# A fused two-layer transformer step on one core: the order of the last three expert blocks and of the work around their gate-up matmuls

## The chip, the cores and the metric

One core of a Trainium2 chip. The metric is the device time of one execution of the whole kernel in microseconds (us), the median over runs.

## The reference

Two layers over 384 tokens (three tiles of 128: one tile of context tokens, two of latent tokens) of width 1024. Each layer has a mixer (retention, windowed attention and neighbourhood attention with one input and one output projection) and then a mixture of experts. The change lies in the second part:

```python
xp = layer_norm(ALPHA * xp + g1 * y, ln1_g[l], ln1_b[l])
f = moe_ffn(xp * (1.0 + sc2) + sh2, w_router[l], b_router[l], w_expert_gu[l],
            w_expert_down[l], w_shared_gu[l], w_shared_down[l])
xp = layer_norm(ALPHA * xp + g2 * f, ln2_g[l], ln2_b[l])
...
def expert_block(args):
    tok, e = args
    gu = x[tok] @ w_gu[e]
    return (jax.nn.silu(gu[:, :D_EXPERT]) * gu[:, D_EXPERT:]) @ w_down[e]
```

There are 64 experts of hidden width 256 (gate-up weights of 2 MB and down weights of 1 MB each), and each token goes to 6 of them. All 64 experts' weights are read from HBM in each layer, so a layer moves about 201 MB in this part. The sum f of a token is its six weighted expert rows and a shared expert's row.

## The kernel before

**Blocks.** The experts are ranked by how many tokens they have, and packed by rank into NB = 29 blocks of 128 rows (`plan_blocks`). A block of one kind holds one expert (128 rows), of another two (64 rows each), a third kind three experts (64, 32 and 32 rows), a fourth two (96 and 32). The experts have a load number n in the order in which blocks use them, 0 to 63. In the kernel before, the last blocks hold: block 24 loads 53 to 55, block 25 loads 56 and 57, block 26 loads 58, 59 and 60, block 27 loads 61 and 62, block 28 load 63.

**A block's work.** For block b: POOL gathers the 128 token rows from memory (L2187); PE transposes them (`turn_rows`, L1118), ACT copies them out (L2099, L2100); PE multiplies by gate and up (`gate_up`, L1141); ACT takes silu (L2107) and DVE the product with the slot's weight (`hidden`, L1617); PE transposes that (`turn_hidden`, L1153), DVE copies (`hidden_turned`, L1626); PE multiplies by down into banks 5 and 6 (`down_rows`, L1168); ACT takes the high part of the two halves (`rows_high`, L2115) and DVE the low part (`rows_out`, L1849). Then the rows are summed back to tokens by a 0/1 matrix (`token_rows`, L1822): six units (three token tiles times two halves f of 512 columns), each unit two matmuls, of the high and of the low part. For blocks 0 to 25 (`add_rows`, L1193 and L1194), PE writes a unit into a bank and DVE adds it to the accumulator in SBUF (`add_unit`, L1835). For the last three (KEPT = 26, 27, 28; `sum_rows`, L1218 and L1219) the six units are kept in six banks (SUM_BANK) and PE accumulates over the three blocks.

**The steady loop.** In iteration b PE runs, in program order: `gate_up(b)`, `add_rows(b-2)` four units, `turn_rows(b+1)`, the other two units, `down_rows(b-1)`, `turn_hidden(b)`. Each engine runs its own list in order; semaphores join them.

**The queue of SP.** The gate-up weights lie in a ring of NG = 4 buffers, the down weights in ND = 6. SP asks for load n of gate-up (L704) when the gate-up matmuls of the block that used load n-4 are done, and for down weights n (L708) when the down matmuls of the block that used load n-6 are done, both in one list in program order: for each b first the down weights of block b, then the gate-up weights whose buffer block b freed. In layer 0 the first two chunks of the next layer's input projection follow (L759), when the blocks of loads 60 and 61 are done.

**The end of a layer.** After `gate_up(28)` PE does units 0 and 1 of block 26's sum, `turn_hidden(28)`, a branch on a value in SBUF (taken only if an expert has more tokens than its room; not taken here), `down_rows(27)`, the rest of block 26's sum, `down_rows(28)`, the sums of block 27 and of block 28. DVE: `gate_sum(0)` to `gate_sum(2)` (L1841, L1842: accumulator times gate plus ALPHA times x) in iteration 27, then hidden of 28, the branch, rows of 27 and 28, and then for each of the three tiles two units, each a product with the gate out of the bank (L1928) and an add (L1929), the statistics of the norm (L1545 to L1548) and the scale and shift of the tile before (L1553, L1554). ACT normalizes a tile (L2072 square root, L2074 scale). POOL does gain and bias of tile 0 (L2233, L2235) and DVE those of tiles 1 and 2 (`residual`, L1800, L1801), after which SP stores them (L781, last layer) or the next layer begins.

Of the kernel before, what the change touches and what calls it, by code (L numbers as in the profile page):

```python
# [43 lines left out]
def plan_blocks():  # L44
# [6 lines left out]
    for kind in (2, 4, 3) * 6 + (2, 3, 4, 3, 2, 3, 2, 1):  # L51
        if kind == 1:
            blocks.append([(next(single), P)])
        elif kind == 4:
            blocks.append([(next(wide), 96), (next(third), 32)])
        elif kind == 2:
            blocks.append([(next(half), 64), (next(half), 64)])
        else:
            blocks.append([(next(half), 64), (next(third), 32), (next(third), 32)])
# [20 lines left out]
OVER_BANK = [0, 2, 3, 4, 5, 6]  # L80
KEPT = NB - 3
# [121 lines left out]
def build(nc, a, o):  # L203
    soft = [(m, t, h) for t in range(TILES) for m in "BC" for h in (0, 3)]

    with ExitStack() as ctx:
# [154 lines left out]
        lo_of = [ys_lo] * (NB - 2) + [rounded("lo_m", "arena_b", DM, DM), ys_lo]  # L361
# [73 lines left out]
        def run_layer(l):  # L435
# [52 lines left out]
            pool_scaled, pool_residual = sem("pool_scaled"), sem("pool_residual")  # L488
# [84 lines left out]
            def _(sp):  # L573
# [200 lines left out]
                else:  # L774
                    for t in range(TILES):
                        if t == 0:
                            sp.wait_ge(pool_residual, 1)
                        else:
                            sp.wait_ge(residual_ready, TILES + t)
# [6 lines left out]
            def _(pe):  # L786
# [369 lines left out]
                def down_rows(b):  # L1156
# [8 lines left out]
                    for f in range(2):  # L1165
                        for k in range(2):
                            for n, r, w in block_tiles(b):
                                ins = pe.matmul(psum[5 + f][r:r + w, :], hT[b % 2][:, k, r:r + w],  # L1168
                                                down[n % ND][:, k, CH * f:CH * f + CH], start=(k == 0), stop=(k == 1))
                    ins.then_inc(y_full, 1)  # L1170
# [82 lines left out]
                for b in range(NB - 1):  # L1253
# [30 lines left out]
                turn_hidden(NB - 1)  # L1284

                pe.wait_ge(most_ready, 1)
                with pe.If(pe.value_load(most[0:1, 0:1], min_val=0, max_val=TOK + P) > P):
                    pe.wait_ge(hT_ready, NB)
# [35 lines left out]
                if has_next:  # L1324
                    for _ in range(18):
                        pe.matmul(psum[5][:, :], ident, cst[:, 0:CH], start=True, stop=True)
# [3 lines left out]
            def _(dve):  # L1330
# [520 lines left out]
                for b in range(NB - 1):  # L1851
# [8 lines left out]
                    if b:  # L1860
# [63 lines left out]
                def from_units(t, z, g, which):  # L1924
                    for f in range(2):
                        u, cols = 2 * t + f, slice(CH * f, CH * f + CH)
                        dve.wait_ge(added_full, UNITS * KEPT + u + 1)
                        link(dve.tensor_tensor(gated_part, psum[SUM_BANK[u]][:, :], g[:, cols], ALU.mult))  # L1928
                        link(dve.tensor_tensor(z[:, cols], z[:, cols], gated_part, ALU.add))  # L1929
# [7 lines left out]
                dve.wait_ge(residual_ready, 2 * TILES - 1)  # L1937
# [3 lines left out]
            def _(act):  # L1941
# [167 lines left out]
                def rows_high(b):  # L2109

                    act.wait_ge(y_full, b + 1)
                    if b:
                        act.wait_ge(added_full, UNITS * min(b, KEPT))
                    for f in range(2):
                        act.activation(hi_of[b][:, CH * f:CH * f + CH], psum[5 + f][:, :], ACT.Copy).then_inc(ys_high, 1)  # L2115

                rows_turned(0)
                for b in range(NB):
                    gated(b)
# [17 lines left out]

                act.wait_ge(most_ready, 1)
# [10 lines left out]
                for b in (NB - 2, NB - 1):  # L2149
                    rows_high(b)  # L2150
                if has_next:
                    act.wait_ge(preloaded[0], 16)
                    act.wait_ge(y_full, BLOCK_OF[E - NG - 1] + 1)
                    for j in range(2):
                        ks = slice(4 * j, 4 * j + 4)
                        act.activation(win_hi[:, ks, :], ring_view(0)[:, ks, :], ACT.Copy).then_inc(next_hi, 1)

# [6 lines left out]
            def _(pool):  # L2164
# [44 lines left out]
                with pool.If(pool.value_load(most[0:1, 0:1], min_val=0, max_val=TOK + P) > P):  # L2209
                    pool.wait_ge(gu_full, NB)  # L2210
# [67 lines left out]
```

## Time and profile before

| | us |
|---|---|
| median of 3 runs | 1816.51 (1815.33 to 1823.99) |
| the profiled execution | 1824.02 |
| its span, first to last instruction | 1822.3 |
| PE busy | 1611.6 (88%) |
| DVE busy | 789.0 (43%) |
| ACT busy | 374.3 (21%) |
| DMA queue of SP, share of 16 engines | 71.2% |
| mean granted TensorE clock | 0.939 |

The span is what the trace covers; 1.7 us of the execution lie around it. The page's slices show the two expert stages as the two stretches in which the DMA engines are at nine tenths and move over 400 GB/s; layer 0's ends near 934 us, layer 1's is the end of the kernel. A row of the timeline gives an instruction group's start, its duration, its engine and line, and in brackets how long its engine sat idle before it and what ended that.

### The profile page before, as it was taken

The page shows a single profiled execution, that of the slowest core. Times are in us where ns is not written, and L with a number is a line of the kernel's source. Part 1 is how long each engine was busy: PE and PEld are TensorE (multiplying, and loading weights), DVE is VectorE, ACT ScalarE, POOL GpSimd, SP SyncE. Part 2 cuts the span into 40 slices and gives each one's busy share as a digit, 9 for nine tenths or more (in the row PEclk, how much of TensorE's full clock was granted, in tenths as well). Part 3 has the DMA queues.
Part 4 walks back from the last instruction along what each step waited for, and adds up shares of the span by engine and source line. Part 5 has one row for each costly group of instructions (what it writes and reads, how often), then busy time and mean ns, then how long its engine had stood idle before and what let it go on. Part 6 is the DMA issues. An engine that isn't in the chain of part 4 may idle for free. (4 is left out here: it accounts for less than half of the span.)

```text
span 1822.3 us, 23929 instructions
## 1 busy us (share of the span) xinstructions
PE 1611.6 (88%) x9205; PEld 847.7 (47%) x9205; DVE 789.0 (43%) x1598; ACT 374.3 (21%) x724; POOL 101.3 (6%) x96
## 2 busy tenths in 40 slices
PE   3999999999998898788979999899999989986884
PEld 1785664544444343333448756555344434332332
DVE  1435433764334334223583444177443433432336
ACT  1323541211111111111232324320111111111111
POOL 0000000110000000000010000001000000000001
PEclk8999989899999999888989999998999999998987
DMA  9535536669999999999634444373799999999980
GB/s 362 183 111 179 189 110 237 271 250 382 423 405 402 414 415 423 396 412 391 252 122 131 150 178 121 112 298 145 300 410 405 402 425 413 417 400 407 402 351 35
DMA packets 101394, 538.93 MB, mean 296 GB/s; under 512 B 34782, under 2 KB 37614, under 8 KB 61980
## 3 DMA queue, kind: packets, MB, share of 16 engines
q1 hardware_dynamic: 91996, 515.24, 71.2%
q0 software_dynamic: 9216, 22.04, 3.2%
q8 instruction: 76, 1.25, 0.3%
q14 instruction: 42, 0.34, 0.1%
q10 hardware_dynamic: 64, 0.07, 0.0%
HBM read 542.73 MB, written 6.55 MB: 301 GB/s over the span
## 5 line engine op out<-in xcount | busy, mean ns | idle before, releaser
L1141 PE MATMUL bank<-ring,arena_a 128*32 128x512 f32 (+2 forms) x2976 | 445.3, 641 | 110.3 <-DMA ring<-in_w_expert_gu 107.3
L1141 PEld LDWEIGHTS bank<-ring,arena_a 128*32 128x32 f32 (+2 forms) x2976 | 137.0, 124 | 391.7 <-issue 388.1
L1617 DVE SCALAR_TENSOR_TENSOR arena_a<-arena_a,slot_w,bank 128x256 f32<-128x256 f32 x58 | 27.9, 480 | 471.2 <-ACT arena_a L2107 365.8
L1835 DVE TENSOR_TENSOR arena_a<-arena_a,bank 128x512 f32<-128x512 f32 x300 | 205.7, 686 | 8.7
L1168 PE MATMUL bank<-arena_b,arena_a 128*32 128x512 f32 (+2 forms) x1040 | 189.3, 595 | 4.9 <-DVE arena_a L1626 2.0
L1193 PE MATMUL bank<-ys_hi,to_token 128*128 128x512 f32 x312 | 132.8, 426 | 0.0
L2107 ACT ACTIVATE arena_a<-bank 128x256 f32<-128x256 f32 x58 | 22.3, 384 | 536.8 <-PE bank L1141 536.8
L1194 PE MATMUL bank<-ys_lo,to_token 128*128 128x512 f32 x312 | 123.2, 395 | 0.0
L900 PE MATMUL bank<-win_hi,xmT_hi 128*128 128x512 f32 (+1 forms) x288 | 109.9, 382 | 15.0 <-DVE arena_a L1370 10.6
L1849 DVE TENSOR_TENSOR ys_lo<-bank,ys_hi 128x512 fp32r<-128x512 f32 x108 | 69.6, 685 | 120.9 <-ACT ys_hi L2115 120.8
L2187 POOL DMA_INDIRECT arena_a<-scratch_x,slot_idx x58 | 62.2, 1073 | 948.3 <-PE bank L1118 838.5
L902 PE MATMUL bank<-w_lo,xmT_hi 128*128 128x512 f32 (+1 forms) x288 | 109.6, 380 | 0.0
L901 PE MATMUL bank<-win_hi,xmT_lo 128*128 128x512 f32 (+1 forms) x288 | 109.2, 379 | 0.0
L1168 PE MATMUL bank<-arena_a 128*32 128x512 f32 (+1 forms) x448 | 101.7, 595 | 1.9 <-issue 0.7
L2115 ACT ACTIVATE ys_hi<-bank 128x512 fp32r<-128x512 f32 x108 | 58.6, 595 | 201.7 <-PE bank L1168 201.7
L1168 PEld LDWEIGHTS bank<-arena_b,arena_a 128*32 128x32 f32 (+2 forms) x1040 | 56.4, 116 | 84.0 <-issue 81.5
L1046 PE MATMUL bank<-ring,xmT 128*128 128x512 f32 x192 | 86.3, 613 | 6.4 <-ACTq L2067 6.4
L1351 DVE TENSOR_TENSOR w_lo<-ring,win_hi 128x2048 fp32r<-128x2048 f32 (+1 forms) x24 | 51.0, 2128 | 81.1 <-ACT win_hi L1973 79.1
L1193 PEld LDWEIGHTS bank<-ys_hi,to_token 128*128 128x128 f32 x312 | 58.6, 188 | 52.4 <-issue 43.1
L2099 ACT ACTIVATE arena_a<-bank 128x512 f32<-128x512 f32 x58 | 34.7, 598 | 178.7 <-PE bank L1118 178.7
L900 PEld LDWEIGHTS bank<-win_hi,xmT_hi 128*128 128x128 f32 x288 | 55.4, 192 | 25.6 <-issue 15.0
L1118 PE MATMUL bank<-cst,arena_a 128*128 128x128 f32 x464 | 62.0, 278 | 3.5 <-DMA arena_a<-scratch_x,slot_idx 3.5
(311 smaller groups left out, 1928.2 us busy)
## 6 DMA issues: line engine op xcount, KB each, us to landing
ring<-in_w_expert_gu SPq DMA_DIRECT2D x128, 2048.0 KB, 13.6
arena_b<-in_w_expert_down SPq DMA_DIRECT2D x88, 1024.0 KB, 18.0
ring<-in_w_mod SPq DMA_DIRECT2D x24, 2048.0 KB, 7.9
arena_a<-in_w_expert_down SPq DMA_DIRECT2D x40, 1024.0 KB, 17.6
ring<-in_w_in SPq DMA_DIRECT2D x10, 2048.0 KB, 12.8
ring<-in_w_out SPq DMA_DIRECT2D x4, 2048.0 KB, 8.0
arena_b<-mods SPq DMA_DIRECT2D x8, 512.0 KB, 11.5
arena_a<-mods SPq DMA_DIRECT2D x8, 512.0 KB, 10.1
```

Source lines behind the costliest of these rows:

```text
L900: pe.matmul(out, hi[:, k, :], win_hi[:, k, cols], start=(k == 0), stop=False)
L901: pe.matmul(out, lo[:, k, :], win_hi[:, k, cols], start=False, stop=False)
L902: ins = pe.matmul(out, hi[:, k, :], w_lo[s][:, k, cols], start=False, stop=(k == KD - 1))
L1046: ins = pe.matmul(bank[:, :], xmT[:, k, P * t:P * t + P], w[:, k, :], start=(k == 0), stop=(k == KD - 1))
L1118: ins = pe.transpose(psum[2 + k // 4][:, P * (k % 4):P * (k % 4) + P], rows_in[:, P * k:P * k + P], ident)
L1141: ins = pe.matmul(psum[0][r:r + w, :], xT[:, k, r:r + w], ring_view(gu_slot(n))[:, k, :], start=(k == 0), stop=(k == KD - 1))
L1168: ins = pe.matmul(psum[5 + f][r:r + w, :], hT[b % 2][:, k, r:r + w], down[n % ND][:, k, CH * f:CH * f + CH], start=(k == 0), stop=(k == 1))
L1193: pe.matmul(bank[:, :], rows_of, ys_hi[:, cols], start=True, stop=False)
L1194: pe.matmul(bank[:, :], rows_of, ys_lo[:, cols], start=False, stop=True).then_inc(added_full, 1)
L1835: ins = dve.tensor_tensor(z, z, bank[:, :], ALU.add)
L1849: dve.tensor_tensor(lo_of[b][:, cols], psum[5 + f][:, :], hi_of[b][:, cols].bitcast(F32), ALU.subtract).then_inc(ys_ready, 1)
L2187: pool.indirect_dma_start(rows_in, None, scratch_x, bass.IndirectOffsetOnAxis(ap=slot_idx[:, b:b + 1], axis=0), bounds_check=TOK - 1, oob_ ...
```

## The change

Seven edits, all in the expert part:

1. The last blocks are in another order: block 26 holds one expert (load 58), block 27 two (59, 60), block 28 three (61, 62, 63).
2. PE: the sums of blocks 26 and 27 (units 0 to 3) and `down_rows(27)` come before `gate_up(28)`; their units 4 and 5 come around `turn_hidden(28)` and `down_rows(28)`. Block 28's sum takes the three units of half 0 first (LAST_UNITS), and each half of a block's rows has a wait of its own (`ys_ready`, `y_half`).
3. ACT: `rows_high(27)` before the silu of block 28; in the last block the high part of half 0 is taken when that half of `down_rows` is done.
4. DVE: in iteration 27 no gate_sum; after it `token_rows(27)`, `gate_sum(0)`, `gate_sum(1)`, `rows_out(27)`, `token_rows(28)`, `gate_sum(2)`, then block 28's own steps, and then all six units (product and add) one after the other, ahead of the statistics.
5. The overflow branch stands behind all sums on every engine (on DVE between the units and the statistics).
6. Gain and bias of tile 0 are done by DVE (`residual(0)`), no longer by POOL.
7. Block 28's low part has a place of its own (`lo_n`).

```diff
-    for kind in (2, 4, 3) * 6 + (2, 3, 4, 3, 2, 3, 2, 1):
+    for kind in (2, 4, 3) * 6 + (2, 3, 4, 3, 2, 1, 2, 3):
...
+LAST_UNITS = [0, 2, 4, 1, 3, 5]
...
+                        if b == NB - 1 and f == 0:
+                            ins.then_inc(y_half, 1)
...
-                            pe.wait_ge(ys_ready, 2 * (b + 1))
+                        pe.wait_ge(ys_ready, 2 * b + 1 + f)
...
+                sum_rows(KEPT, range(4))
+                down_rows(NB - 2)
+                sum_rows(NB - 2, range(4))
                 gate_up(NB - 1)
-                sum_rows(KEPT, range(2))
                 turn_hidden(NB - 1)
+                sum_rows(KEPT, [4])
+                sum_rows(NB - 2, [4])
+                down_rows(NB - 1)
+                sum_rows(KEPT, [5])
+                sum_rows(NB - 2, [5])
+                sum_rows(NB - 1, LAST_UNITS)
...
-                down_rows(NB - 2)
-                sum_rows(KEPT, range(2, UNITS))
-                down_rows(NB - 1)
-                sum_rows(NB - 2, range(UNITS))
-                sum_rows(NB - 1, range(UNITS))
...
-                        if b == KEPT + 1:
-                            dve.wait_ge(norm_loaded, 128)
-                            gate_sum(0)
                         rows_out(b - 1)
                     hidden_turned(b)
-                    if b == KEPT + 1:
-                        gate_sum(1)
-                        gate_sum(2)
...
+                dve.wait_ge(xT_full, NB)
+                token_rows(NB - 2)
+                dve.wait_ge(norm_loaded, 128)
+                gate_sum(0)
+                gate_sum(1)
+                rows_out(NB - 2)
+                token_rows(NB - 1)
+                gate_sum(2)
                 hidden(NB - 1)
                 hidden_turned(NB - 1)
+                rows_out(NB - 1)
+
+                for i, u in enumerate(LAST_UNITS):
+                    t, f = u // 2, u % 2
+                    cols = slice(CH * f, CH * f + CH)
+                    dve.wait_ge(added_full, UNITS * KEPT + i + 1)
+                    dve.tensor_tensor(gated_part, psum[SUM_BANK[u]][:, :], gateb[:, 0 if t == 0 else 1, cols], ALU.mult).then_inc(units_read, 1)
+                    dve.wait_ge(units_read, i + 1)
+                    link(dve.tensor_tensor(xm[:, t, cols], xm[:, t, cols], gated_part, ALU.add))
...
-                for b in (NB - 2, NB - 1):
-                    token_rows(b)
-                    rows_out(b)
...
+                for t in range(TILES):
+                    statistics(1, t, summed)
                     if t:
-                        scale_shift(which, t - 1)
-
-                norm(1, from_units)
+                        scale_shift(1, t - 1)
+                dve.wait_ge(normal_ready, TILES + 1)
+                residual(0)
+                scale_shift(1, TILES - 1)
                 for t in range(1, TILES):
                     dve.wait_ge(normal_ready, TILES + t + 1)
                     residual(t)
-                dve.wait_ge(residual_ready, 2 * TILES - 1)
+                dve.wait_ge(residual_ready, 2 * TILES)
...
                 for b in range(NB):
+                    if b == NB - 1:
+                        rows_high(NB - 2)
                     gated(b)
...
-                pool.wait_ge(normal_ready, TILES + 1)
-                pool.tensor_tensor(xm[:, 0, :], xm[:, 0, :], lnb[:, 0, :], ALU.mult).then_inc(pool_scaled, 1)
-                pool.wait_ge(pool_scaled, 1)
-                pool.tensor_tensor(x[:, 0, :], xm[:, 0, :], lnb[:, 1, :], ALU.add).then_inc(pool_residual, 1)
-                pool.wait_ge(pool_residual, 1)
```

## Rows read from the trace of the kernel before

**Rows 1.** The page, busy time, share and instructions of each engine.

```profile
PE 1611.6 (88%) x9205; PEld 847.7 (47%) x9205; DVE 789.0 (43%) x1598; ACT 374.3 (21%) x724; POOL 101.3 (6%) x96
```

**Rows 2.** Timeline of PE, layer 1: gate-up of block 25, hidden turned, gate-up of 26.

```profile
1718.97 7.09 PE L1141 MATMUL bank<-ring,arena_a 128*64 128x512 f32 x32 [0.71 <-DMA ring<-in_w_expert_gu]
...
1733.62 0.44 PE L1153 MATMUL bank<-cst,arena_a 128*128 128x128 f32 x2
1741.27 9.67 PE L1141 MATMUL bank<-ring,arena_a 128*32 128x512 f32 x64 [7.21 <-DMA ring<-in_w_expert_gu]
```

**Rows 3.** Timeline, layer 1: gate-up of blocks 27 and 28.

```profile
1759.95 7.09 PE L1141 MATMUL bank<-ring,arena_a 128*64 128x512 f32 x32 [1.06 <-DMA ring<-in_w_expert_gu]
...
1774.79 7.03 PE L1141 MATMUL bank<-ring,arena_a 128*128 128x512 f32 x16
```

**Rows 4.** Timeline of PE, layer 0: gate-up of blocks 23, 26, 27 and 28.

```profile
792.46 7.07 PE L1141 MATMUL bank<-ring,arena_a 128*32 128x512 f32 x64 [2.41 <-DMA ring<-in_w_expert_gu]
...
854.26 9.44 PE L1141 MATMUL bank<-ring,arena_a 128*32 128x512 f32 x64 [7.56 <-DMA ring<-in_w_expert_gu]
872.20 7.09 PE L1141 MATMUL bank<-ring,arena_a 128*64 128x512 f32 x32 [0.53 <-DMA ring<-in_w_expert_gu]
887.04 7.03 PE L1141 MATMUL bank<-ring,arena_a 128*128 128x512 f32 x16
```

**Rows 5.** SP's gate-up weight issues, layer 1, and their time from issue to landing.

```profile
1711.00 2.54 SPq L704 DMA_DIRECT2D ring<-in_w_expert_gu  x3
1726.80 1.43 SPq L704 DMA_DIRECT2D ring<-in_w_expert_gu  x2
...
DMA to landing us min/median/max: 7.8/13.0/18.1
```

**Rows 6.** One window, layer 1: us, busy PE, PEld, DVE, ACT, POOL, clock, DMA share, GB/s.

```profile
1734.00:1741.00 7.00, 0.06 (x1) 0.00 (x0) 1.62 (x3) 0.83 (x2) 0.00 (x0) 0.67 1.00 420
```

**Rows 7.** Timeline, layer 1: block 26's high and low parts, half a gate_sum.

```profile
1774.64 1.08 ACT L2115 ACTIVATE ys_hi<-bank 128x512 fp32r<-128x512 f32 x2 [3.54 <-PE bank L1168]
...
1775.34 1.29 DVE L1849 TENSOR_TENSOR ys_lo<-bank,ys_hi 128x512 fp32r<-128x512 f32 x2
...
1780.65 1.22 DVE L1842 SCALAR_TENSOR_TENSOR arena_a<-x,arena_a 128x1024 f32<-128x1024 f32 x1
```

**Rows 8.** Timeline, layer 1, from the last gate-up on.

```profile
1781.86 0.38 ACT L2107 ACTIVATE arena_a<-bank 128x256 f32<-128x256 f32 x1 [6.13 <-PE bank L1141]
...
1784.25 3.65 PE L1168 MATMUL bank<-arena_b,arena_a 128*64 128x512 f32 x16 [0.93 <-DVE arena_a L1626]
...
1784.56 0.68 DVE L1822 TENSOR_SCALAR to_token<-cst,slot_tok 128x128 fp32r<-128x128 f32 x3 [0.78 <-issue]
...
1796.24 0.39 PE L1218 MATMUL bank<-hi_n,to_token 128*128 128x512 f32 x1
...
1796.69 0.39 PE L1218 MATMUL bank<-hi_n,to_token 128*128 128x512 f32 x1
```

**Rows 9.** Timeline, layer 1: the end.

```profile
1796.89 0.69 DVE L1928 TENSOR_TENSOR rows<-bank,arena_b 128x512 f32<-128x512 f32 x1 [1.30 <-PE bank L1219]
...
1797.62 0.69 DVE L1929 TENSOR_TENSOR arena_a<-arena_a,rows 128x512 f32<-128x512 f32 x1
...
1806.09 2.34 POOL L2233 TENSOR_TENSOR arena_a<-arena_a,arena_b 128x1024 f32<-128x1024 f32 x1 [75.34 <-ACT arena_a L2074]
...
1806.99 1.99 DVE L1929 TENSOR_TENSOR arena_a<-arena_a,rows 128x512 f32<-128x512 f32 x1
...
1814.39 1.22 DVE L1800 TENSOR_TENSOR arena_a<-arena_a,arena_b 128x1024 f32<-128x1024 f32 x1
...
1818.04 1.23 DVE L1801 TENSOR_TENSOR x<-arena_a,arena_b 128x1024 f32<-128x1024 f32 x1
```

**Rows 10.** Timeline of DVE, layer 0: behind the branch, and the last one.

```profile
897.12 0.68 DVE L1822 TENSOR_SCALAR to_token<-cst,slot_tok 128x128 fp32r<-128x128 f32 x3 [1.08 <-issue]
...
930.42 1.23 DVE L1801 TENSOR_TENSOR x<-arena_a,arena_b 128x1024 f32<-128x1024 f32 x1
```

More of the change, by code:

```diff
@@ L360, in build @@
         hi_of = [ys_hi] * (NB - 2) + [rounded("hi_m", "arena_b", DM, 0), rounded("hi_n", "arena_a", DM, xg_at + DM)]
-        lo_of = [ys_lo] * (NB - 2) + [rounded("lo_m", "arena_b", DM, DM), ys_lo]
+        lo_of = [ys_lo] * (NB - 2) + [rounded("lo_m", "arena_b", DM, DM), rounded("lo_n", "arena_a", DM, xg_at + 2 * DM)]
         over_rows = xg[1]
@@ L487, in run_layer @@
             rows_cleared = sem("rows_cleared")
-            pool_scaled, pool_residual = sem("pool_scaled"), sem("pool_residual")
+            y_half, units_read = sem("y_half"), sem("units_read")
             early_ready, mod_used = sem("early_ready"), sem("mod_used")
@@ L775, in _ @@
                     for t in range(TILES):
[L776 to L779, printed above, removed]
+                        sp.wait_ge(residual_ready, TILES + t + 1)
                         dst = o["y_prompt"][0] if t == 0 else o["y_sample"][0, P * (t - 1):P * t, :]
@@ L1281, in _ @@
                         shared(*SHARED_AT[b])
+                sum_rows(KEPT, range(4))
+                down_rows(NB - 2)
+                sum_rows(NB - 2, range(4))
                 gate_up(NB - 1)
-                sum_rows(KEPT, range(2))
                 turn_hidden(NB - 1)
+                sum_rows(KEPT, [4])
[4 more added lines that the diff above has]
+                sum_rows(NB - 1, LAST_UNITS)
+                if has_next:
+                    for _ in range(18):
+                        pe.matmul(psum[5][:, :], ident, cst[:, 0:CH], start=True, stop=True)
                 pe.wait_ge(most_ready, 1)
                 with pe.If(pe.value_load(most[0:1, 0:1], min_val=0, max_val=TOK + P) > P):
-                    pe.wait_ge(hT_ready, NB)
+                    pe.wait_ge(units_read, UNITS)
                     for q in range(PASSES):
@@ L1317, in _ @@
                     pe.wait_ge(over_added, PASSES * E)
-                down_rows(NB - 2)
-                sum_rows(KEPT, range(2, UNITS))
-                down_rows(NB - 1)
-                sum_rows(NB - 2, range(UNITS))
-                sum_rows(NB - 1, range(UNITS))
-                if has_next:
-                    for _ in range(18):
-                        pe.matmul(psum[5][:, :], ident, cst[:, 0:CH], start=True, stop=True)
             @blk.vector
@@ L1918, in _, with summed @@
                     dve.nop()
-                for b in (NB - 2, NB - 1):
-                    token_rows(b)
-                    rows_out(b)
[L1924 to L1929, printed above, removed]
+                def summed(t, z, g, which):
+                    pass
+                for t in range(TILES):
+                    statistics(1, t, summed)
                     if t:
-                        scale_shift(which, t - 1)
-                norm(1, from_units)
+                        scale_shift(1, t - 1)
+                dve.wait_ge(normal_ready, TILES + 1)
+                residual(0)
+                scale_shift(1, TILES - 1)
                 for t in range(1, TILES):
@@ L2109, in rows_high @@
                 def rows_high(b):
-                    act.wait_ge(y_full, b + 1)
+                    if b < NB - 1:
+                        act.wait_ge(y_full, b + 1)
                     if b:
@@ L2114, in rows_high @@
                     for f in range(2):
+                        if b == NB - 1:
+                            act.wait_ge(y_full if f else y_half, NB if f else 1)
                         act.activation(hi_of[b][:, CH * f:CH * f + CH], psum[5 + f][:, :], ACT.Copy).then_inc(ys_high, 1)
@@ L2118, in _ @@
                 for b in range(NB):
+                    if b == NB - 1:
+                        rows_high(NB - 2)
                     gated(b)
@@ L2136, in _ @@
                         act.activation(sg_s, psum[7][:, 0:F], ACT.Silu).then_inc(ssilu_done, 1)
+                rows_high(NB - 1)
+                if has_next:
+                    act.wait_ge(preloaded[0], 16)
+                    act.wait_ge(y_full, BLOCK_OF[E - NG - 1] + 1)
+                    for j in range(2):
+                        ks = slice(4 * j, 4 * j + 4)
+                        act.activation(win_hi[:, ks, :], ring_view(0)[:, ks, :], ACT.Copy).then_inc(next_hi, 1)
                 act.wait_ge(most_ready, 1)
@@ L2148, in _ @@
                     act.nop()
[L2149 to L2156, printed above, removed]
                 norm(1, *range(TILES))
@@ L2209, in _ @@
                 with pool.If(pool.value_load(most[0:1, 0:1], min_val=0, max_val=TOK + P) > P):
-                    pool.wait_ge(gu_full, NB)
+                    pool.wait_ge(units_read, UNITS)
                     pool.wait_ge(table_empty, 16)
```

## The prediction

> **What bounds the kernel now.** I read the page first: PE is busy for 88% of the span [rows 1], so PE is the bound where it works, and the question is where it doesn't. Then the waits of PE and the timeline around the last blocks of each layer, then SP's issues, then the end of the layer engine by engine. Two things are to be seen.
>
> First, in the expert stage PE and the weight stream are nearly in balance. A plain iteration takes 15.1 us when nothing holds PE (gate-up of block 25 starts at 1718.97, and PE is free for the next one at 1741.27 - 7.21 = 1734.06) [rows 2]. Block 26 then waits 7.21 us for its third expert's weights [rows 2], while the DMA engines are full at 420 GB/s and the granted clock falls to 0.67, and its gate-up, behind the idle time, takes 9.67 us, where others take 7.1 [rows 2, 3, 6]: part of it runs at 1.2 instead of 2.4 GHz. Layer 0 has the same wait at the same block: 7.56 us, then 9.44 us [rows 4]. Block 27 waits another 1.06 and 0.53 us [rows 3, 4].
>
> Second, behind the last gate-up a serial tail is left. In layer 1 the gate-up of block 28 ends at about T = 1781.85 (silu starts at 1781.86) [rows 8]. The first product of the final sums comes at 1796.89, T + 15.0, and DVE is then the chain to 1819.27, 22.4 us long [rows 9]. Stores make the rest.
>
> **The change part by part.**
>
> *The order of the blocks.* SP asks for load n when load n-4's block is done. Loads 57 to 59 are asked for behind block 24 (issue at 1711.00), 60 and 61 behind block 25 (1726.80) [rows 5]. Before, block 26 needs load 60, which lands at 1741.27, 14.5 us after its issue. After, block 26 needs load 58 alone. Load 57 had landed by 1718.97, 8 us after its issue [rows 2, 5], and from there to 1741.27 the stream carried 22.3 us x 0.42 MB/us = 9.4 MB, which is 58, 59, 60 and three down weights. In order, 58 lands near 1724 to 1729, before 1734.06. So block 26 starts when PE is free, at 1734.1, with no idle time and at the full clock. Block 27 needs load 60, in by 1741.3, and PE comes to it at 1734.1 + 15.0 = 1749.1: no wait. It ends at S = 1749.1 + 7.1 = 1756.2, where before it ended at 1767.05 [rows 3]: 10.9 us earlier (7.2 wait + 2.6 clock + 1.1 wait). In layer 0: PE is free for block 26 at 846.7, S = 846.7 + 15.0 + 7.1 = 868.8 against 879.3: 10.5 us [rows 4].
>
> *The price of that order.* Load 62 is now asked for behind block 26 and load 63 behind block 27, at S + 0.6; before, both behind block 26. Then down weights 61 to 63 queue on SP behind 63, and in layer 0 the two chunks of the next layer's projection (the second only behind the last gate-up; it has the 30 us of the tail). The stream has, from 1741.3: loads 61 and 62 and downs 58 to 60, 7.3 MB, 17.5 us at 0.42, so to 1759; then 63 (5 us) to about 1764 = S + 8, then three downs to 1772. Issue to landing was 7.8 to 18.1 us in this stretch [rows 5], so 63 lands between S + 8.4 and S + 18.7; I take S + 9, by the bytes.
>
> *What moves ahead of the last gate-up.* Before, 7.74 us lay between the end of block 27's gate-up and the start of block 28's (1767.05 to 1774.79) [rows 3]. Now: PE ends turn_hidden(27) at about S + 7.9. Block 26's low part comes in halves at S + 8.9 and S + 9.5 (ACT's high part starts at S + 7.6, DVE's 0.65 each) [rows 7]. A unit is 0.45 us of PE [rows 8], so units 0 to 3 end at S + 10.9. down_rows(27) takes 3.65 [rows 8]: S + 14.55. Meanwhile DVE makes the 0/1 rows (0.7) and two gate_sums (four of 1.22 to 1.25 [rows 7], 5.0) from S + 9.85 to S + 15.55; rows_out(27) is queued behind them, and PE waits for it. ACT's first half is there at S + 15.2, so the gate_sums cost 0.3 us. Low parts at S + 16.2 and 16.85, four units: block 28's gate-up starts at S + 18.3. That is 10.5 us more than before. PE idles there 1.0 and 1.7 us. Load 63 is in by then. The start is at 1756.2 + 18.3 = 1774.5 (before 1774.79: -0.3) in layer 1, and 868.8 + 18.3 = 887.1 (before 887.04: +0.1) in layer 0. So the gain of the block order pays for the moved work, nearly to the microsecond. The last block's kind doesn't matter: 7.03 to 7.09 us for one, two or three experts [rows 3, 4].
>
> *Behind the last gate-up.* Silu, product, transposes and copy let down_rows start at T + 2.4 [rows 8], as before; gate_sum(2) on DVE ends at S + 20, under the gate-up. Units 4 of both blocks fill the wait (0.9 us). down_rows(28): T + 2.4 to T + 6.0. Its first half is taken by ACT and DVE under the second one; the second costs 0.6 + 0.65 [rows 7]: T + 7.35. PE does units 5 (0.9) and then the first unit of block 28 meanwhile, done at about T + 7.4, and is faster than DVE from there (0.45 against 1.45 a unit). So DVE's first product is at T + 7.45, where it was T + 15.0: -7.55.
>
> *DVE's chain.* It was 22.4 us [rows 9]. The six units and statistics stay. The branch is now in it: 0.78 or 1.08 us of issue [rows 8, 10]. The two adds that took 2.0 us while POOL worked go back to 0.69: -2.6 [rows 9]. residual(0) comes in: 4.88 / 2 = +2.45 (1814.39 to 1819.27 is two of them) [rows 9]. About 0.3 us of waiting for ACT's root at the end goes, since residual(0) covers it. Bounds: the branch costs nothing less than 0.78 and, as it is read once from SBUF with nothing queued over it, I allow up to 2. Together +0.3 to +1.7; I take +0.5. ACT's normalization of tile 0 (1.24) lies under the statistics of tile 2 (1.6).
>
> **Sum.** Per layer -7.55 + 0.5 = -7.05 in the tail; starts -0.3 and +0.1: -14.3 us over both layers. Layer 1's start (barrier behind 931.65 [rows 10]) just moves. Profiled execution 1824.0 -> 1809.7. It was 7.5 us above the median of the runs, so against that median: 1816.5 - 14.3 = 1802.2. I say 1802.
>
> **A rule on the clock.** The row says: 2.41 us of idle ahead of a gate-up left it at 7.07 us, 7.56 us of idle made it 9.44 [rows 4]; so I take the new idle times of 1.0 and 1.7 us as free. The Trainium skill (TensorE: Matmul & The Clock Gate, "A second HAM failure mode: psum-queue depth-cycling") says that short idle times between groups of matmuls can be enough to make the clock go back and forth, though no single one is long. By that rule the last gate-up would run in part at 1.2 GHz; rival A is worked out for it from the rows.
>
> **Rivals.**
>
> A. *The last gate-up loses the clock.* Two idle times within 10 us ahead of it, 2.7 us together. For: the dependence of the sums on ACT and DVE is new. Against: 2.41 us in one piece did nothing [rows 4]. Price 9.55 - 7.05 = 2.5 us a layer: 1807.
>
> B. *The stall moves instead of going* (the side of slower). If loads 58 to 60 share the engines and land together near 1741, or if load 63 lands past S + 18.3, the wait only changes its block, while 10.5 us of work has moved ahead of the last gate-up. For: 7.8 to 18.1 us to landing [rows 5]. Against: load 57 took 8 us with 58 and 59 issued right behind it, and 8 us is enough for about 3 MB, not for 6. Price: with block 26 at 1741.3 and 9.6 us long, block 27 ends at 1766 and the last gate-up starts at 1784: +9.5 and +10 in the two layers, less 14.1 in the tail: +5.4 us, 1822. With load 63 at 18.7 us behind its issue in both layers besides, 1 us of wait each, and the clock (2.5 each): +12.4, 1829. It decides from a landing of load 58 past 1734 + 7. The Trainium skill (DMA: Bandwidth & Descriptors, "Queues, rings and completion order") says that completion isn't first in, first out for one issuing engine; the row of load 57 speaks for near order.
>
> C. *DVE's chain is longer*: the branch is dearer on the path than the issue gaps show, or two adds stay at 2.0 us for another reason than POOL. For: nothing waited for the branch alone before. Against: the two slow adds lie inside POOL's work and the one of 1797.62 outside it took 0.69 [rows 9]. Price: 1.2 and 2.6 us a layer: 1802 + 7.6 = 1810.
>
> **Chances.** Forecast (1796 to 1807) 0.70; A 0.08; B 0.12 (0.05 of it partial, near 1812, 0.04 near 1822, 0.03 near 1829); C 0.05; better than 1796, since removed idle time may also help the clock and stream around it, 0.05. Bounds of the unknown costs: load 63 (0 to 3 us), branch (up to 1.2 a layer), run-to-run spread of stalls (the shown runs lie 8.7 us apart): 1795 to 1812. 0.5% of the time, 9.1 us, is about what a measurement of this kernel can tell from no change. Faster by that (under 1807.4): 0.76; within: 0.16; slower (over 1825.6): 0.08.
>
> **What would show each step.** Gate-up of block 26 (x16) with no wait and at 7.0 us; block 27 (x32) without one; 18.3 us between the end of block 27's gate-up and the start of block 28's (x64), with no DMA as the releaser, in 7.05 us; first L1928-like product 7.5 us behind its end; all six adds at 0.69; DVE's chain 22.9 us. Wrong would make it: a DMA wait ahead of any of the three last gate-ups, above all load 63; a duration over 9 us for the last one; DVE's low parts of block 27 later than S + 17.

## The result, and the profile after

The changed kernel runs in 1811.4 us (median of 20 runs, 1804.2 to 1823.0) against 1820.3 us of the kernel before (20 runs beside them): ratio 0.9954, 95% interval 0.9933 to 0.9974. Two further sets, on other occasions, gave 0.9945 (0.9923 to 0.9967) and 0.9929 (0.9900 to 0.9959). Over all sets the mean of 41 runs is 9.3 +- 1.9 us below the mean of 95 runs of the kernel before (1812.2 and 1821.5). The forecast was 14.3 us below 1816.5, the median of the three runs known then: 1802 us.

The profiled execution took 1805.2 us, 18.8 less than the profiled one of before. That is no measure of the change: at the first row below it is 12.0 us ahead, 6.9 us of it from the end of layer 0, which the edits touch, and 5.1 us from code that no edit touches. What can be compared is the stretch that the edits touch. PE's timeline of the changed kernel, layer 1, with the gate-up matmuls of blocks 25 to 28 (L1139 now) and the first sums (L1218) of blocks 26 and 27, each with DVE's low parts (L1851) above it:

```profile
1706.95 7.09 PE L1139 MATMUL bank<-ring,arena_a 128*64 128x512 f32 x32 [0.89 <-DMA ring<-in_w_expert_gu]
...
1721.79 7.03 PE L1139 MATMUL bank<-ring,arena_a 128*128 128x512 f32 x16
...
1736.68 7.09 PE L1139 MATMUL bank<-ring,arena_a 128*64 128x512 f32 x32
...
1752.07 1.29 DVE L1851 TENSOR_TENSOR ys_lo<-bank,ys_hi 128x512 fp32r<-128x512 f32 x2 [2.44 <-ACT ys_hi L2127]
1752.86 0.48 PE L1218 MATMUL bank<-ys_hi,to_token 128*128 128x512 f32 x1 [1.24 <-issue]
...
1759.41 1.29 DVE L1851 TENSOR_TENSOR lo_m<-bank,hi_m 128x512 fp32r<-128x512 f32 x2 [0.23 <-ACT hi_m L2127]
1760.25 0.47 PE L1218 MATMUL bank<-hi_m,to_token 128*128 128x512 f32 x1 [1.58 <-DVE lo_m L1851]
...
1762.31 7.07 PE L1139 MATMUL bank<-ring,arena_a 128*32 128x512 f32 x64
1770.47 0.44 PE L1151 MATMUL bank<-cst,arena_a 128*128 128x128 f32 x2 [1.08 <-DVE arena_a L1619]
```

Block 26 (x16) and block 27 (x32) start without a wait and at the full clock, where the kernel before waited 7.21 and 1.06 us and took 9.67 for block 26 [rows 2, 3]. The two new idle times ahead of the last gate-up are there, 1.24 and 1.58 us (1.0 and 1.7 were predicted), and it keeps the clock: 7.07 us. For the 1.24 us the profile names no releaser; by the times it is the first of DVE's two low parts of block 26, which ends about 0.1 us ahead of the sum. For the 1.58 us DVE is named, and DVE itself had waited 0.23 us for ACT's high part, so the gate_sums queued ahead of it cost nothing (0.3 us was predicted). From the end of block 27's gate-up (1743.77) to its start it is 18.5 us, 7.74 before; 18.3 was predicted. Load 63 doesn't hold it. SP's issue of load 63, and its time to landing:

```profile
1744.52 0.33 SPq L705 DMA_DIRECT2D ring<-in_w_expert_gu  x1
...
DMA to landing us min/median/max: 8.3/8.3/8.3
```

It lands 9.0 us behind the end of block 27's gate-up. The last rows, from the silu of block 28 (ACT L2116) on: DVE's first product of the final units (L1892), the statistics behind the branch (L1547), and the last instruction.

```profile
1769.45 0.38 ACT L2116 ACTIVATE arena_a<-bank 128x256 f32<-128x256 f32 x1 [9.66 <-PE bank L1139]
...
1777.01 0.69 DVE L1892 TENSOR_TENSOR rows<-bank,arena_b 128x512 f32<-128x512 f32 x1 [0.22 <-PE bank L1219]
...
1784.98 0.69 DVE L1894 TENSOR_TENSOR arena_a<-arena_a,rows 128x512 f32<-128x512 f32 x1
1786.94 1.29 DVE L1547 BATCH_NORM_STATS2 cmisc<-arena_a 128x6 f32<-128x512 f32 x2 [1.27 <-issue]
...
1798.82 1.23 DVE L1803 TENSOR_TENSOR x<-arena_a,arena_b 128x1024 f32<-128x1024 f32 x1
```

The first product comes 7.56 us behind the start of block 28's silu, which the prediction took as the end of the gate-up (15.0 before [rows 8, 9]), all adds take 0.69, the branch shows as 1.27 us in which DVE waits for nothing that the profile shows, and DVE's chain is 23.0 us (22.4 before [rows 9]). 7.45 and 22.9 were predicted.

To compare traces I cut each layer at the start of the silu of blocks 25, 27 and 28 and at the end of DVE's last instruction. Each number is a difference of two such times, in us; two numbers are the two layers. All traces taken for this study are in it (the kernels are told below).

| trace | untouched rest of the span | silu 25 to 27 | silu 27 to 28 | silu 28 to end | touched stretch |
|---|---|---|---|---|---|
| before | 1636.3 | 40.5, 41.0 | 14.8, 14.8 | 37.5, 37.4 | 92.8, 93.2 |
| before, 2nd | 1625.7 | 39.3, 40.5 | 14.8, 14.8 | 37.5, 37.4 | 91.7, 92.7 |
| before, 3rd | 1633.6 | 42.4, 41.1 | 14.8, 14.8 | 37.6, 37.4 | 94.8, 93.3 |
| changed | 1631.2 | 29.8, 29.7 | 25.7, 25.6 | 30.5, 30.6 | 85.9, 86.0 |
| changed, 2nd | 1634.0 | 29.8, 29.8 | 25.7, 25.7 | 30.5, 30.6 | 86.0, 86.0 |
| changed, 3rd | 1645.9 | 29.8, 29.8 | 25.7, 25.7 | 30.5, 30.6 | 85.9, 86.0 |
| order alone | 1648.7 | 29.7, 29.7 | 16.1, 16.2 | 37.8, 37.6 | 83.7, 83.6 |
| order alone, 2nd | 1636.6 | 29.8, 29.7 | 15.6, 16.0 | 37.9, 37.6 | 83.2, 83.3 |
| order alone, 3rd | 1635.9 | 29.7, 29.7 | 15.7, 15.8 | 37.9, 37.5 | 83.3, 83.1 |
| order in layer 0 | 1642.3 | 29.7, 41.5 | 15.5, 14.8 | 37.8, 37.4 | 83.1, 93.7 |
| order in layer 1 | 1637.1 | 40.8, 29.7 | 14.8, 15.9 | 37.6, 37.6 | 93.1, 83.2 |
| all but the order | 1644.9 | 40.4, 41.1 | 25.4, 25.4 | 30.2, 30.3 | 96.0, 96.8 |
| sum 27 behind | 1636.9 | 29.8, 29.8 | 21.9, 21.9 | 31.3, 31.4 | 83.0, 83.1 |
| sum 27 behind, 2nd | 1636.6 | 29.8, 29.8 | 21.9, 21.9 | 31.3, 31.4 | 82.9, 83.0 |
| no branch | 1638.0 | 29.8, 29.8 | 25.7, 25.6 | 29.5, 29.5 | 84.9, 84.8 |
| POOL does tile 0 | 1634.5 | 29.7, 29.9 | 25.7, 25.7 | 31.6, 31.7 | 87.1, 87.2 |

The touched stretch is 93.2 us before (mean of the eight stretches that have the old program and the old order) and 86.0 after: 7.2 us a layer, 14.4 in all. From one execution to another it varies by 0.1 us in the changed kernel and by 3.1 us in the kernel before, where the stall lies in it. The rest of the span, in which every kernel does the same, varies by 23 us.

### The profile page after: what moved, and what is told of

Its sections match the earlier page's. It is cut to its first block and busy times, and to the rows that moved or that the text cites. A ratio compares the mean times of both kernels' runs of the same rounds, so it can differ in the third digit from the quotient of the medians.

```text
span 1803.1 us, 23939 instructions
## 1 busy us (share of the span) xinstructions
PE 1600.1 (89%) x9205; PEld 842.2 (47%) x9205; DVE 790.0 (44%) x1602; ACT 373.9 (21%) x724; POOL 91.8 (5%) x92
## 5 line engine op out<-in xcount | busy, mean ns | idle before, releaser
L1139 PE MATMUL bank<-ring,arena_a 128*32 128x512 f32 (+2 forms) x2976 | 441.3, 636 | 97.0 <-DMA ring<-in_w_expert_gu 93.7
L1139 PEld LDWEIGHTS bank<-ring,arena_a 128*32 128x32 f32 (+2 forms) x2976 | 136.4, 123 | 374.2 <-issue 370.3
L1166 PE MATMUL bank<-arena_b,arena_a 128*32 128x512 f32 (+1 forms) x1056 | 181.9, 595 | 3.3 <-issue 1.0
L2116 ACT ACTIVATE arena_a<-bank 128x256 f32<-128x256 f32 x58 | 22.3, 384 | 524.8 <-PE bank L1139 524.8
L1851 DVE TENSOR_TENSOR ys_lo<-bank,ys_hi 128x512 fp32r<-128x512 f32 x108 | 69.6, 686 | 125.4 <-ACT ys_hi L2127 125.4
L1166 PE MATMUL bank<-arena_a 128*32 128x512 f32 (+2 forms) x432 | 109.1, 595 | 1.9 <-issue 0.7
L1166 PEld LDWEIGHTS bank<-arena_b,arena_a 128*32 128x32 f32 (+1 forms) x1056 | 53.4, 115 | 79.5 <-issue 78.6
## 6 DMA issues: line engine op xcount, KB each, us to landing
ring<-in_w_in SPq DMA_DIRECT2D x10, 2048.0 KB, 10.8
```

The lines of the kernel that those rows point to most:

```text
L1139: ins = pe.matmul(psum[0][r:r + w, :], xT[:, k, r:r + w], ring_view(gu_slot(n))[:, k, :], start=(k == 0), stop=(k == KD - 1))
L1851: dve.tensor_tensor(lo_of[b][:, cols], psum[5 + f][:, :], hi_of[b][:, cols].bitcast(F32), ALU.subtract).then_inc(ys_ready, 1)
```

## The experiments

**The block order alone, and all but the block order.** The first is the kernel before with this line, the second the changed kernel with this line undone:

```diff
-    for kind in (2, 4, 3) * 6 + (2, 3, 4, 3, 2, 3, 2, 1):
+    for kind in (2, 4, 3) * 6 + (2, 3, 4, 3, 2, 1, 2, 3):
```

> The kernel before with edit 1 alone (last three blocks hold one, two and three experts; PE, DVE, ACT and POOL programs as before). Theory M (the block order carries the whole gain, the moved sums give some of it back): block 26 no longer waits 7.2 us, its gate-up takes 7.0 us instead of 9.5 to 9.7; load 63 is asked for 0.7 us behind the end of block 27's gate-up and lands 8.3 us later, so block 28's gate-up starts 9.0 us behind it and not 7.74: +1.3 us of DMA wait. 10.7 - 1.3 = 9.4 us a layer, -19 us in all, and faster than the changed kernel by about 5 us. Rival R (the moved sums are what pays, they are needed to hide load 63): the wait for load 63 is 5 us or more and its gate-up loses the clock; the kernel is at or above the changed one. Rival N (in most executions the stall at block 26 is smaller than in the profiled one): gain under 12 us.

> The changed kernel with edit 1 undone (block order of before, all the rest of the change kept). Theory M: block 26's wait of 7 us and its slow gate-up are back; from the end of block 27's gate-up it takes 18.5 us to block 28's and 56.2 us to DVE's last instruction, where the kernel before took 52.2: slower than before by 4 us a layer, +8 us. Rival R (the moved sums pay by themselves): faster than before by 5 us or more.

Order alone: ratio 0.9916 (0.9884 to 0.9948). All but the order: 1.0022 (0.9997 to 1.0047), mean of 12 runs 6.4 +- 3.6 us above all runs of before and 5.0 +- 4.0 us above those on its own chip; the ratio alone doesn't tell it from no change, the traces do. In the traces the order alone takes 83.3 us (mean of its eight stretches in the table) where the whole change takes 86.0, and the rest alone 96.4: theory M, with 9.9 gained and 3.2 lost a layer. PE's rows of the order alone (its second trace, layer 1), hidden turned of block 27 and the gate-up of block 28:

```profile
1753.86 0.38 PE L1153 MATMUL bank<-cst,arena_a 128*128 128x128 f32 x2
1755.29 7.07 PE L1141 MATMUL bank<-ring,arena_a 128*32 128x512 f32 x64 [1.05 <-DMA ring<-in_w_expert_gu]
```

Load 63, asked for as late as in the changed kernel, costs 1.05 us here (0.70 to 1.29 us in the six layers of the three traces) and the gate-up behind it takes 7.07 us in all six. That is all that the moved sums had to hide. The whole change pays 10.9 us for them ahead of the last gate-up (25.7 against 14.8 from silu 27 to silu 28) and gets 6.9 back behind it. All but the order shows the old stall again, 7.48 us and a gate-up of 9.67:

```profile
1753.26 9.67 PE L1139 MATMUL bank<-ring,arena_a 128*32 128x512 f32 x64 [7.48 <-DMA ring<-in_w_expert_gu]
1771.85 7.09 PE L1139 MATMUL bank<-ring,arena_a 128*64 128x512 f32 x32 [0.96 <-DMA ring<-in_w_expert_gu]
```

Rival R is out for both kernels. The expected -19 us is within the interval of the times (-21 to -9), near its end. Beside each other on one chip the order alone is 5.0 +- 4.6 us faster than the changed kernel.

**The changed kernel and the kernel before again.** No edit.

> The changed kernel once more, for its time beside the other two on one chip and for a second trace. Forecast of the prediction: -14 us against before. Rival N (the stall removed is smaller in most executions): -5 to -10 us, and in the trace the stretch from block 25's gate-up to DVE's last instruction is again 93 us in both layers, so the missing part lies ahead of it or in the kernel before.

> The kernel before once more, for a second trace. Prediction: the stretch from the start of block 25's gate-up to DVE's last instruction is again 100 us in both layers, with 7 us of wait at block 26. Rival N: that wait is under 4 us, its gate-up keeps the clock, and the stretch is under 96 us.

Ratio 0.9945 (0.9923 to 0.9967). The kernel before shows the stall again, 6.4 and 6.9 us of wait at block 26; the changed one shows none. So rival N falls: the stall that was removed is no matter of one lucky trace. The third trace of the kernel before shows it too, 7.72 and 7.55 us. The whole still came out at -10 us, as rival N had it for another reason, and the stretch at -14.

**The sum of block 27 behind the last gate-up.** The changed kernel with one line moved:

```diff
-                sum_rows(NB - 2, range(4))
                 gate_up(NB - 1)
+                sum_rows(NB - 2, range(4))
                 turn_hidden(NB - 1)
```

> The changed kernel with one line moved: PE does units 0 to 3 of block 27's sum behind the last gate-up and not ahead of it, so that the 1.6 us wait for block 27's low part and the 1.9 us of sums lie beside ACT's and DVE's work on block 28. Theory M (idle time and work put ahead of the last gate-up is what the moved sums cost): from the end of block 27's gate-up to block 28's silu 22 us instead of 25.7 (the last gate-up starts at 14.8 us and load 63, there at 9.0, doesn't hold it), behind it 0.9 us more, so 2.8 us a layer less than the changed kernel, 5.6 in all; about as fast as the block order alone or 1 us faster. Rival R (the gate-up needs the sums ahead to hide load 63): a DMA wait appears ahead of the last gate-up and the gain is under 1 us.

Ratio 0.9887 (0.9850 to 0.9924). 21.9 us from silu to silu and 31.35 behind it: 3.0 us a layer less than the changed kernel, as worked out. Its PE rows in layer 1:

```profile
1755.69 0.47 PE L1218 MATMUL bank<-ys_hi,to_token 128*128 128x512 f32 x1 [1.24 <-issue]
...
1761.42 7.07 PE L1139 MATMUL bank<-ring,arena_a 128*32 128x512 f32 x64
1768.43 0.50 PE L1218 MATMUL bank<-hi_m,to_token 128*128 128x512 f32 x1
...
1770.39 0.38 PE L1151 MATMUL bank<-cst,arena_a 128*128 128x128 f32 x2
```

The gate-up follows down_rows(27) at once, with no DMA wait, the 1.58 us of idle time is gone, and the four units fill the time in which ACT and DVE make block 28's hidden rows (1.08 us of PE idle time in the changed kernel). A second set, beside the changed kernel:

> The changed kernel a third time. The traces so far give 6.7 us a layer for the stretch that the change touches (block 25's silu to DVE's last instruction: 92.6 before, 86.0 after), 13.3 us in all, and the times so far -9 and -10. If the missing 4 us are scatter of the stretches that no edit touches (layer starts of 324 to 339 us, blocks 0 to 25 of 464 to 471 us), the difference here is as likely above as below 13 us, and the three sets together come nearer to it. If something outside the stretch is made slower, it is -9 to -10 again.

> The kernel with the sum of block 27 behind the last gate-up again, beside the changed kernel on one chip. By the traces: 83.0 against 86.0 us a layer, so 6 us faster than the changed kernel and 19 us faster than before.

The changed kernel: 0.9929 (0.9900 to 0.9959). With the sum behind: 0.9926 (0.9892 to 0.9960). The traces agree with the ones before to 0.1 us (83.0 and 86.0), but the times don't separate the two: 2.2 +- 5.6 us, where 6 was expected, and 14 us below before, where 19 was. Over both sets the kernel with the sum behind is 15.3 +- 3.2 us below before.

**No branch.** The changed kernel with the overflow blocks removed on all five engines (`with dve.If(...)` and its like); it leaves out the overflow experts' part. One execution; only its trace is used, as for the experiment behind it.

> The changed kernel without the branch for overflowing experts on any engine (this part of the computation is left out; it isn't taken with these inputs). The prediction took 0.8 to 1.1 us for it on DVE's chain; the changed kernel's trace shows 1.17 and 1.27 us of issue there. Expected: that gap goes to under 0.1 us in both layers and DVE's chain from the first product of the last units is 21.8 us instead of 23.0. If the gap stays, it is the norm's start that costs it and not the branch.

DVE's last add and the statistics behind it, layer 1 (L1853 and L1506 here), to be read against 1784.98 and 1786.94 of the changed kernel:

```profile
1790.77 0.69 DVE L1853 TENSOR_TENSOR arena_a<-arena_a,rows 128x512 f32<-128x512 f32 x1
1791.49 1.29 DVE L1506 BATCH_NORM_STATS2 cmisc<-arena_a 128x6 f32<-128x512 f32 x2
```

The gap is gone and the stretch 1.1 us shorter in each layer. So the branch, which isn't taken, costs 1.1 to 1.3 us where it lies on DVE's chain. Before, DVE had cover for its own: it waited 3.33 us more for ACT behind it. PE had none: its branch lay between `turn_hidden(28)` and `down_rows(27)`, where PE sits idle for 0.93 us in all three traces of before [rows 8]. The view puts that down to a DVE copy, but the rows that `down_rows(27)` reads were long there. So some of the 7.5 us gained behind the last gate-up may be this branch going off PE's way; no run here separates it.

**POOL does tile 0.** The changed kernel with edit 6 undone:

```diff
-                dve.wait_ge(normal_ready, TILES + 1)
-                residual(0)
                 scale_shift(1, TILES - 1)
...
-                dve.wait_ge(residual_ready, 2 * TILES)
+                dve.wait_ge(residual_ready, 2 * TILES - 1)
...
+                pool.wait_ge(normal_ready, TILES + 1)
+                pool.tensor_tensor(xm[:, 0, :], xm[:, 0, :], lnb[:, 0, :], ALU.mult).then_inc(rows_cleared, 1)
+                pool.wait_ge(rows_cleared, PREB + 1)
+                pool.tensor_tensor(x[:, 0, :], xm[:, 0, :], lnb[:, 1, :], ALU.add).then_inc(slots_ready, 1)
+                pool.wait_ge(slots_ready, 2)
```

> The changed kernel with edit 6 undone: POOL does gain and bias of tile 0 beside DVE, as before. The prediction: POOL's 5 us slow down DVE's instructions with two inputs in SBUF beside it by up to 2.9 times (0.69 to 2.0 us in the kernel before). POOL's work now lies beside the gain and bias of tile 1: expected 2.4 us saved on DVE and about as much lost there, end of the layer within 1 us of the changed kernel. Rival: no slowing, 2.4 us a layer shorter.

1.15 us a layer longer than the changed kernel (87.15 against 86.0), just outside the 1 us expected. Layer 1, POOL's second instruction and DVE's ahead of it, beside it and behind it:

```profile
1798.50 0.16 DVE L1558 RECIPROCAL cmisc<-cmisc 128x1 f32<-128x1 f32 x1 [1.40 <-ACT cmisc L2082]
...
1798.93 3.31 POOL L2249 TENSOR_TENSOR x<-arena_a,arena_b 128x1024 f32<-128x1024 f32 x1
...
1800.07 3.25 DVE L1806 TENSOR_TENSOR x<-arena_a,arena_b 128x1024 f32<-128x1024 f32 x1
...
1803.24 1.21 DVE L1805 TENSOR_TENSOR arena_a<-arena_a,arena_b 128x1024 f32<-128x1024 f32 x1
1804.49 1.22 DVE L1806 TENSOR_TENSOR x<-arena_a,arena_b 128x1024 f32<-128x1024 f32 x1
```

The same DVE instruction takes 3.25 us beside POOL and 1.22 without it, and DVE waits 1.40 us for ACT's root, which residual(0) had covered. The rival without slowing is out, and edit 6 is worth 1.15 us.

**The order alone again, and in one layer alone.** The first has no new edit. The other two keep a table of ranks and blocks for each layer (`ends = (new, old)` or `(old, new)` in `plan_blocks(l)`), and are otherwise the kernel before.

> The kernel with edit 1 alone once more, for its time and a second trace. Theory M: -15 to -19 us against before, ahead of the changed kernel by 5; in the trace 123.5 us again from block 23's silu to the layer's end. Open question: in its first trace layer 1's mixer, which no edit touches, took 331 us from the end of layer 0 to the first silu, where five other traces show 317 to 321. If that comes with the earlier end of layer 0 it is there again; if it is a matter of the single execution it is 317 to 321 now.

> The kernel before a third time, for a trace: the touched stretch 92 to 93 us in both layers; the rest of the span is 1626 to 1649 us in ten traces of all kernels, so 1636 +- 7 here too if it is scatter.

> The kernel before with the new block order in layer 0 alone (layer 1 keeps its own). Touched stretch: 83.5 us in layer 0, 92.6 in layer 1. If the earlier end of layer 0 makes layer 1's start slower (by about 5 us), the whole is 4 to 5 us faster than before; if not, 9 us.

> The kernel before with the new block order in layer 1 alone. Touched stretch: 92.6 us in layer 0, 83.5 in layer 1. Nothing ahead of layer 1's last blocks differs from the kernel before, so by the rival that layer 1's start is what loses the whole 9 us must arrive; if the gain is again some 2 us short of the stretch in both kernels, the shortfall is scatter or lies in each expert stage.

> The block order in both layers, beside the two halves on one chip. Stretch 83.5 us in both layers, -18 us by the traces; -14 and -20 us in the two sets so far.

The order alone: 0.9891 (0.9855 to 0.9928), then 0.9911 (0.9879 to 0.9943). Layer 1's start, from DVE's last instruction of layer 0 to the silu of block 0, was 326.5 us in the second trace and 327.6 in the third, where the first had 339.2 (the expectations read it to ACT's table load, 7 to 8 us ahead of that silu: 331, and 317 to 321 in the others). So that was the single execution. The kernel before, third trace: stretch 94.8 and 93.3, rest 1633.6. Order in layer 0 alone: 0.9968 (0.9947 to 0.9989), -7.6 +- 3.3 us; in layer 1 alone: 0.9951 (0.9929 to 0.9972), -9.4 +- 2.5 us. That is against all runs of before; against the 23 on their own chip it is -6.1 +- 3.7 and -7.9 +- 2.9 us, and -16.6 +- 4.4 for the order in both layers. The two halves differ by less than their errors: a loss at layer 1's start, which would have cost the first one 5 us and the second none, is neither shown nor excluded.

## Why the prediction was right or wrong

**The steps inside the stretch were right.** The layer's gain was put together as 10.5 to 10.9 us from the order (measured: 40.9 to 29.8 from silu 25 to silu 27, 11.1), 10.5 us paid ahead of the last gate-up (10.8 between the gate-ups, 10.9 between the silus), 7.55 gained behind it (7.5) and 0.5 lost on DVE's chain (0.6). Sum forecast 14.3, measured in the traces 14.4. The bounds for load 63 (8.4 to 18.7 us behind block 27) held it at the lower end, 9.0, as taken.

**Rival A** (the clock is lost by short idle times) is out in every trace: 1.24 and 1.58 us of idle time, then 7.07 us. By the Trainium skill's rule on many short idle times (TensorE: Matmul & The Clock Gate, "A second HAM failure mode: psum-queue depth-cycling") it might have been otherwise; these two did nothing. The row that the prediction took as proof, 2.41 us of idle time and then 7.07 us [rows 4], was thinner than it looked. In layer 1 of the same trace two idle times of nearly one length are followed by different gate-ups, ahead of blocks 5 and 23:

```profile
1330.71 8.45 PE L1141 MATMUL bank<-ring,arena_a 128*32 128x512 f32 x64 [2.73 <-DMA ring<-in_w_expert_gu]
...
1680.28 7.08 PE L1141 MATMUL bank<-ring,arena_a 128*32 128x512 f32 x64 [2.69 <-DMA ring<-in_w_expert_gu]
```

So the length of an idle time alone didn't settle the clock, and that the last gate-up kept it is shown by its own rows, not by the one that the forecast leaned on: some luck was in it. **Rival B** (the stall moves) is out: no DMA wait ahead of any of the last three gate-ups. Its concern, loads landing together, doesn't show: load 58 is in time for block 26 in every trace with the new order. The trace of before could have settled it: there loads 57, 58 and 59, issued within 2.2 us, land 7.8, 13.0 and 16.8 us behind their issues, load 58 at 1725.1, 9 us before PE is free. **Rival C** was half present: the branch costs 1.2 us on the path and not 0.8, the adds were as predicted.

**What failed is the last line of the sum**: "against that median: 1816.5 - 14.3 = 1802.2". Both of its terms were off. The median of three runs stood for the kernel before; 20 runs gave 1820.3, 3.8 us more. And the 14.3 us of the stretch were taken as the fall of the whole, which is 8.9 us by the medians of this set, 5.4 us less. Together that is the 9.2 us between 1802.2 and 1811.4. The second term weighs more: had the 14.3 us arrived in full, 1820.3 - 14.3 = 1806.0 would have been inside the range. Over all sets the whole fell by 9.3 +- 1.9 us, so 5 us of what the stretch shows don't arrive, and the chance of 0.76 for more than 0.5% rested on it; the measured ratios lie on both sides of 0.995. The stretch and the times of all kernels, in us against before (mean of all runs with its 95% interval):

| kernel | runs | stretch, both layers | time |
|---|---|---|---|
| changed | 41 | -14.4 | -9.3 +- 1.9 |
| order alone | 21 | -19.7 | -15.9 +- 2.6 |
| sum 27 behind | 13 | -20.3 | -15.3 +- 3.2 |
| order in layer 0 | 12 | -10.1 | -7.6 +- 3.3 |
| order in layer 1 | 12 | -10.0 | -9.4 +- 2.5 |
| all but the order | 12 | +6.5 | +6.4 +- 3.6 |

The shortfall is 4 to 5 us wherever the new order is in both layers, 2.5 and 0.6 with it in one, nothing without it. In the changed kernel it is clear of the intervals of its times and of the stretch, so chance alone is a poor account of it. The runs tell in part what goes with it. Each has the mean granted clock of its span. I take from it the stretch (its length and clock from the traces) and get the clock of the rest:

| kernel | runs with a clock | clock of the rest of the span |
|---|---|---|
| before | 75 | 0.9451 +- 0.0009 |
| all but the order | 12 | 0.9448 +- 0.0023 |
| order in layer 1 | 12 | 0.9452 +- 0.0015 |
| order in layer 0 | 12 | 0.9437 +- 0.0024 |
| order alone | 21 | 0.9432 +- 0.0016 |
| sum 27 behind | 13 | 0.9429 +- 0.0021 |
| changed | 41 | 0.9426 +- 0.0012 |

Among the runs of any one kernel, 0.001 less of this clock goes with 1.1 to 1.4 us more. By that, an estimate, the 0.0025 between before and changed stand for 3 us of the shortfall. Another 0.4 us lies around the span: 2.1 us in the changed kernel and 1.7 before. The remaining 1.7 us are about as large as the errors. So most of what doesn't arrive goes with a lower granted clock in code that no edit touches. What lowers it isn't shown, and neither is the place. One candidate is layer 1's start, 326.2 us on average in the five traces with the old order in layer 0 and 328.8 in the eleven with the new one; but with a range of 324 to 339 us these can't be told from chance.

**What the prediction didn't ask.** It priced the block order and the moved sums, found that they cancel ahead of the last gate-up, and never set down the case of the order without the sums, though all its terms were there: S + 9.0 for load 63, not S + 18.3, and the old tail. Of the change's own edits that case keeps the one that gains (9.9 us a layer) and drops the others, which together lose 2.7 us beside it. One line of them explains the whole loss: with the four units of block 27's sum put behind the last gate-up, 3.0 us come back. Ahead of it these units and the 1.58 us wait for their low part delay the gate-up; behind it they fill time in which PE waits anyway. What they could hide was 0.7 to 1.3 us.

The fastest kernels here are the order alone and the change with the sum of block 27 behind the last gate-up: 1805.6 and 1806.2 us on average against 1812.2 of the changed kernel and 1821.5 of before. The two aren't told apart (0.5 +- 3.6 us beside each other on one chip).

## What to carry to other kernels

When a change bundles a reordering that removes a stall with moves that are to pay for its side effect, price the reordering alone first, with the side effect at its own size: here a weight that came 0.7 to 1.3 us late was hidden at a net cost of 2.7 us a layer. Moving work ahead of a wait gains only what the wait is long, and each dependence that thereby comes to lie in the open (here the low parts that wait for ACT's high parts, 1.58 us, and a branch between sums and norm, 1.2 us) is paid in full. And of a program whose untouched parts scatter by 20 us, compare like stretches of several traces, and give the whole-kernel forecast a range that doesn't rest on the stretch alone, nor on a base of three runs.

## What the runs showed of the hardware

The same code can take 324 to 339 us at the start of layer 1 (from DVE's last instruction of layer 0 to the silu of block 0), and the longest start has the lowest granted clock (0.90 against 0.93 to 0.95 in the other traces). Two windows of the kernel before and the like two of the order alone (first trace), 120 to 160 and 220 to 240 us behind the end of layer 0; columns are us, busy time with counts for PE, weight loads, DVE, ACT and POOL, then clock, DMA share and GB/s:

```profile
1051.60:1091.60 40.00, 37.20 (x243) 21.50 (x242) 18.19 (x53) 11.02 (x36) 2.89 (x6) 0.96 0.49 184
1151.60:1171.60 20.00, 14.09 (x91) 10.71 (x92) 2.52 (x8) 12.29 (x25) 0.00 (x0) 0.95 0.06 21
```

```profile
1042.70:1082.70 40.00, 38.26 (x206) 20.82 (x205) 14.21 (x41) 5.79 (x15) 2.90 (x6) 0.70 0.30 109
1142.70:1162.70 20.00, 20.00 (x99) 14.00 (x99) 3.77 (x12) 7.06 (x20) 0.00 (x0) 0.66 0.00 1
```

The program is the same in both; one execution is granted 0.96 and the other 0.70, and gets through fewer matmuls (206 against 243) in the same time, with PE no less busy. In the second windows it is busy for 20.0 us with 99 matmuls, the other for 14.1 us with 91. Much of the scatter of the times goes with this clock: among the 20 runs of the changed kernel those at a mean clock of 0.948 took 1804 to 1808 us and those at 0.936 to 0.938 took 1821 to 1823. What sets the clock in one execution and not in the next, no run here shows.
